# A two-layer decoder trunk on one core: the second layer's input projections by seven products of half-size blocks

## The chip, the cores and the metric

The kernel runs on one core of one Trainium2 chip. A core has five engines with queues of their own: TensorE (PE, matmuls), VectorE (DVE), ScalarE (ACT), GpSimd (POOL) and SyncE (SP, which issues the DMAs here). They wait for each other by semaphores. The metric is the device time of one execution in microseconds, smaller is better. A "product" below is one matmul instruction that streams 512 columns.

## The reference, cut to what matters

One sequence of 1024 tokens, width 1024, float32. Layer 0 is a gated delta rule branch with short convolutions; the change does not touch its arithmetic. Layer 1 is:

```python
def stick_breaking_branch(h, w_in, w_out):           # layer 1; D_MODEL = 1024, 8 heads of 128
    proj = h @ w_in                                  # w_in: 1024 x 4096
    q, k, v, gate = jnp.split(proj, 4, axis=-1)
    ...
    def block(args):                                 # one block of 128 queries, all keys
        mask = key_pos[None, :] < qpos[:, None]
        z = jnp.einsum('bhqd,bhsd->bhqs', q_blk, k).astype(jnp.float32) * scale
        log_1m = jnp.where(mask, jax.nn.log_sigmoid(-z), 0.0)
        tail = lax.cumsum(log_1m, axis=3, reverse=True) - log_1m
        A = jnp.where(mask, jnp.exp(jax.nn.log_sigmoid(z) + tail), 0.0)
        return jnp.einsum('bhqs,bhsd->bhqd', A.astype(v.dtype), v)
    ...
    return (o * jax.nn.silu(gate)) @ w_out

def reference(...):
    u = rmsnorm(h, norm_w[0]); h = h + gated_deltanet_branch(u, ...)
    u = rmsnorm(h, norm_w[1]); h = h + stick_breaking_branch(u, b_w_in[0], b_w_out[0])
    return rmsnorm(h, final_norm_w)
```

## The kernel before, in words

Activations are kept with channels on the 128 partitions and tokens along the free axis: `xT(cb)` is channel block cb (8 of them, 128x1024). Blocks 0 to 4 stay in `home`; 5 to 7 are in `late` and go through DRAM (`resid`) while other data has the memory.

To reach float32 accuracy every projection is made of three products of parts: a factor is split into an upper part (`w_hi`, `u_hi`, a copy of type fp32r) and a rest (`w_lo`, `u_lo`, the difference), and hi*hi + lo*hi + hi*lo are summed in PSUM (`products`). The uppers of weights are copied by ACT (`split_hi`), the rests subtracted by POOL (`split_lo`); weights have two buffers. So one 128x1024 output takes 2 halves x 8 channel blocks x 3 = 48 products, and the four outputs of a head (query, key, gate, value) 192.

At the end of layer 0, `last_group(i)` adds the last two heads' share of the output, 16 groups of 6 products; DVE adds each to xT (`add_output`), ACT makes the upper part of the next layer's input and its squares, DVE the rest (`u_lower_half`), POOL sums the squares (`add_squares`), and PE sums them over the partitions (`block_sum`), from which ACT makes the inverse norm `rsb`. The products of head 0 run meanwhile; the norm is applied behind them (`scale_qk`, `scale_gate`, `scale_v`).

`attend(h)` works on head h in eight steps s, the longest query block (8 blocks of keys) first. On PE a step is: scores of the block two steps ahead, transposes of the weights, their product with the values (`weigh`), and between them products of the next head's projections, in numbers that the table STEP_FILL gives (4 places a step, 192 in all). On DVE a step is: softplus sum, causal mask, a running sum (`scan`), copies of the transposed weights (`copy_aT`), `exponent`; on ACT three functions for softplus, one exponential. Each engine does its instructions in the order in which the code gives them. `take_b` (ACT) brings a finished half of an output from PSUM to `b_raw`, after 24 products each; there are two PSUM banks for projections, 0 and 1. In step 5 DVE scales queries and keys of the next head (`scale_qk`), which PE needs for its scores in step 6. The last head has no next one: PE does the first output block's products in it. After it come the output projection (`products(("out", cb))`, 8 blocks of 48), the final norm, and the store.

## Time and profile before

| | us |
|---|---|
| median of 3 runs | 1469.81 (1467.81 to 1470.13) |
| profiled execution, its own time | 1469.78 |
| its span, first to last instruction | 1468.1 |
| PE busy | 1386.8 (94%) |
| DVE busy | 903.0 (62%) |
| ACT busy | 640.1 (44%) |
| POOL busy | 435.1 (30%) |

The page gives each engine's busy time and the chain of work that ended last, followed back from the end. Layer 0 fills the span to about 776 us (the first `last_group`), the heads of layer 1 run from there to about 1366 us, the output projection to 1449 us. PE's matmuls overlap in the records; the pitch of a row of them says how long one takes.

### The profile page before, as it was taken

What the parts mean: (1) busy time and instruction counts of PE and PEld (TensorE: products, weight loads), DVE (VectorE), ACT (ScalarE), POOL (GpSimd) and SP (SyncE); (2) the same over time, 40 slices, a digit from 0 to 9 for tenths busy, and PEclk for the clock granted to TensorE, in tenths of its full rate; (3) what the DMA queues carried; (4) which work ended last, traced back from release to release, by engine and by line L of the source; (5) the groups of instructions that cost most, each with busy time, mean ns of one, the idle gap of its engine ahead of it and who ended that gap; (6) DMA issues with size and microseconds to landing.
All of it is one profiled execution on the core that took longest, in us unless ns stands there. A gap on an engine that the chain in (4) does not pass through costs nothing.

```text
span 1468.1 us, 18492 instructions
## 1 busy us (share of the span) xinstructions
PE 1386.8 (94%) x7351; PEld 1135.2 (77%) x7351; DVE 903.0 (62%) x1540; ACT 640.1 (44%) x887; POOL 435.1 (30%) x230
## 2 busy tenths in 40 slices
PE   6898999999999999996998999999999999997896
PEld 4687788888888888885886787878787877875785
DVE  7387787869787878777338255454545555557313
ACT  6153435253535353443235354545454454546113
POOL 6542333323333343335124422111212122111120
PEclk9999999999999999997999999999999999999999
DMA  7211110101111101130111201111111111000302
GB/s 188 58 29 29 29 37 22 50 24 37 30 36 37 36 22 37 33 110 27 65 42 57 72 29 44 29 30 29 29 43 29 30 29 40 27 21 0 115 29 114
DMA packets 97190, 65.20 MB, mean 44 GB/s; under 512 B 2401, under 2 KB 91602, under 8 KB 97106
## 3 DMA queue, kind: packets, MB, share of 16 engines
q1 hardware_dynamic: 97106, 64.04, 14.7%
q8 instruction: 58, 0.95, 0.3%
q14 instruction: 26, 0.21, 0.0%
HBM read 53.54 MB, written 10.49 MB: 44 GB/s over the span
## 4 chain that ended last, share of the span: by engine, by line
PE 80%; DVE 12%; POOL 3%; ACT 2%; issue 2%; DMA 0%; POOLq 0%; SPq 0%; DVEq 0%; PEldq 0%; ACTq 0%
PE psum L408 51%; PE psum L1761 4%; PE psum L1787 4%; DVE terms L1316 3%; POOL acc L637 2%; PE psum L1774 2%; PE psum L1704 2%; PE psum L1649 2%; PE psum L1719 2%; PE psum L1674 2%; PE psum L1695 2%; PE psum L1658 1%; DVE small_L L1301 1%; DVE stick L1444 1%; PE psum L1600 1%
## 5 line engine op out<-in xcount | busy, mean ns | idle before, releaser
L408 PE MATMUL psum<-u_hi,w_hi 128*128 128x512 f32 x1264 | 523.9, 414 | 26.0 <-DVE u_lo L1089 7.2
L408 PE MATMUL psum<-u_lo,w_hi 128*128 128x512 f32 x1264 | 517.2, 409 | 0.0
L408 PE MATMUL psum<-u_hi,w_lo 128*128 128x512 f32 x1264 | 506.6, 401 | 0.0
L381 POOL TENSOR_TENSOR w_lo<-w_raw,w_hi 128x1024 fp32r<-128x1024 f32 (+1 forms) x83 | 213.2, 2568 | 702.8 <-ACT w_hi L376 702.8
L408 PEld LDWEIGHTS psum<-u_hi,w_hi 128*128 128x128 f32 x1264 | 240.5, 190 | 81.9 <-issue 19.7
L408 PEld LDWEIGHTS psum<-u_lo,w_hi 128*128 128x128 f32 x1264 | 240.4, 190 | 51.1 <-issue 7.5
L408 PEld LDWEIGHTS psum<-u_hi,w_lo 128*128 128x128 f32 x1264 | 240.2, 190 | 49.8 <-issue 3.8
L376 ACT ACTIVATE w_hi<-w_raw 128x1024 fp32r<-128x1024 f32 (+1 forms) x83 | 85.8, 1034 | 158.7 <-PE psum L408 103.8
L708 POOL TENSOR_TENSOR Lb<-dec,level 128x512 f32<-128x512 f32 (+1 forms) x64 | 89.0, 1406 | 126.5 <-PE psum L1704 69.2
L1185 DVE SCALAR_TENSOR_TENSOR late<-raw,cols,late 128x1024 f32<-128x1024 f32 x72 | 120.1, 1668 | 1.9
L1028 ACT ACTIVATE soft<-psum 128x1024 f32<-128x1024 f32 (+3 forms) x64 | 41.7, 652 | 154.1 <-DVE psum L1432 153.4
L1432 DVE TENSOR_TENSOR psum<-psum,causal 128x128 f32<-128x128 f32 x64 | 19.1, 298 | 132.8 <-PE psum L1761 132.8
L921 ACT ACTIVATE v_new<-psum 128x128 f32<-128x128 f32 x64 | 17.7, 277 | 188.5 <-PE psum L1620 188.5
L1444 DVE TENSOR_TENSOR_SCAN stick<-soft 128x1024 f32<-128x1024 f32 (+3 forms) x64 | 98.3, 1536 | 0.0
L1459 DVE COPY aT<-psum 128x512 f32<-128x512 f32 (+1 forms) x96 | 52.4, 546 | 69.0 <-PE psum L1774 69.0
L1761 PE MATMUL psum<-b_k,b_q 128*128 128x512 f32 (+1 forms) x192 | 74.2, 495 | 8.3 <-DVE stick L1451 7.9
L1787 PEld LDWEIGHTS psum<-aT,b_v 128*128 128x128 f32 x576 | 75.2, 195 | 4.5
L1206 DVE TENSOR_TENSOR raw<-psum,rsb 128x512 f32<-128x512 f32 x64 | 43.8, 687 | 56.6 <-PE psum L408 56.6
L812 ACT ACTIVATE b_raw<-psum 128x512 f32<-128x512 f32 x64 | 38.0, 594 | 91.0 <-PE psum L408 90.9
L1316 DVE TENSOR_TENSOR terms<-Xs,small_T 128x16 f32<-128x16 f32 (+14 forms) x120 | 71.5, 596 | 9.7 <-DVE small_T L1321 0.5
L1787 PE MATMUL psum<-aT,b_v 128*128 128x128 f32 x576 | 76.0, 278 | 0.0
L1761 PEld LDWEIGHTS psum<-b_k,b_q 128*128 128x128 f32 x192 | 34.7, 188 | 32.6 <-issue 15.3
(212 smaller groups left out, 2032.5 us busy)
## 6 DMA issues: line engine op xcount, KB each, us to landing
w_raw<-in_a_w_in SPq DMA_DIRECT2D x33, 512.0 KB, 4.1
w_raw<-in_b_w_in SPq DMA_DIRECT2D x32, 512.0 KB, 4.0
x_stage<-in_x SPq DMA_DIRECT2D x8, 512.0 KB, 7.3
w_raw<-in_b_w_out SPq DMA_DIRECT2D x8, 512.0 KB, 3.6
out<-fin_o SPq DMA_DIRECT2D x8, 512.0 KB, 2.6
resid<-late SPq DMA_DIRECT2D x6, 512.0 KB, 3.4
o_rows<-o_nrm SPq DMA_DIRECT2D x12, 256.0 KB, 2.0
w_raw<-in_a_w_out SPq DMA_DIRECT2D x8, 384.0 KB, 3.2
```

The lines of the kernel that those rows point to most:

```text
L376: A.activation(tiles(w_hi, key), tiles(w_raw, key), ACT.Copy).then_inc(hi_done, 1)
L381: G.tensor_tensor(tiles(w_lo, key), tiles(w_raw, key), tiles(w_hi, key).bitcast(F32), ALU.subtract).then_inc(lo_done, 1)
L408: mm = PE.matmul(psum[:, half], (w_hi, w_hi, w_lo)[part][:, n % 2, k], (u_hi, u_lo, u_hi)[part][:, k, half * HALF:(half + 1) * HALF], star ...
L708: G.tensor_tensor(Lb[:, g, :, used], half_of(dec, g)[:, :, used], level[:, l:l + 1, used].broadcast_to((P, 4, used.stop)), ALU.mult).then_ ...
L1028: A.activation(soft[:, slot, 0:w], banks(bk)[:, 0:w], ACT.Abs).then_inc(soft_a.handle, 1)
L1185: V.scalar_tensor_tensor(out=conv[:, s], in0=tap, scalar=by, in1=conv[:, s], op0=ALU.mult, op1=ALU.add).then_inc(convs.handle, 1)
L1206: V.tensor_tensor(raw[:, slot, 3 + half * HALF:3 + (half + 1) * HALF], psum[:, half], rsb[:, half_range(half)], ALU.mult).then_inc(proj_ta ...
L1316: V.tensor_tensor(terms[:, :, 0:r + 1], row_L[:, r % 2, :, 0:r + 1], small_T[:, :, 0:r + 1], ALU.mult).then_inc(terms_done.handle, 1)
L1444: V.tensor_tensor_scan(stick[:, slot, 0:w][:, ::-1], soft[:, slot, 0:w][:, ::-1], soft[:, slot, 0:w][:, ::-1], 0.0, ALU.add, ALU.bypass).t ...
L1459: V.tensor_copy(aT[:, s % 2, 4 * g:4 * g + n], bank(6, n)).then_inc(at_done.handle, 1)
L1761: mm = PE.matmul(psum[:, bk + c // HALF, 0:n], b_q[:, qb * P:(qb + 1) * P], b_k[:, c:c + n], start=True, stop=True)
L1787: mm = PE.matmul(psum[:, 7, t], b_v[:, blk, :], aT[:, s % 2, blk], start=blk == 0, stop=blk == qb)
```

## The change: what it does

The four projections of a head are taken as two pairs (query and key; gate and value). A pair's output (2 blocks of 128 columns by 2 halves of 512 tokens) is a 2x2 product of blocks over 2 halves of the 1024 channels, and is computed by Strassen's scheme in Winograd's form: seven block products p1 to p7 instead of eight. A block product is 12 matmul products (4 channel blocks x 3 parts), so a pair takes 84 in place of 96. The first pair of all (head 0, query and key) stays plain.

- **Weights.** The left factors of p5, p6, p7 and p3 are sums and differences of weight blocks, made on POOL (`factor_sums`, three 128x512 instructions a pair, and one behind p2's rest). Each of the 14 factors of a head is split at 128x512: `factor_hi` on ACT, `factor_lo` on POOL, in a ring of four.
- **Inputs.** The right factors of p5, p6, p7 and p4 are sums of quarters of the scaled input: made once, on DVE (`difference_t1`, `sums_t`), and split by ACT, DVE and POOL into `t_hi` and `t_lo`, at the start of layer 1. The squares are now taken and added in halves.
- **Results.** The seven products use two PSUM banks and accumulate on each other; ACT takes two results of a pair, DVE five, each with an add (`take_pair`, 128x512).
- **Keys.** The scaled keys of heads 1 to 7 are made on POOL (`scale_k`) in place of DVE.
- **Order in a head.** STEP_FILL has two places a step, 168 in all; in step 7 DVE copies the transposed weights ahead of the scan; in step 0 it scales the values ahead of the copy; ACT's last exponential of a head stands inside the next head's first softplus.
- **Memory.** `o_raw` lies where the input parts are, so outputs of heads 0 to 6 go to DRAM (`b_rows`) and come back in the last head; all eight residual blocks (before: three) are stored and loaded again ahead of the output projection. A barrier at the start of layer 1 is gone.

```diff
-STEP_FILL = ((4, 8, 6, 23), (4, 8, 5, 11), (4, 6, 4, 10), (4, 5, 3, 9), (4, 5, 0, 8), (4, 4, 0, 6),
-             (2, 1, 0, 0), (4, 4, 14, 22))
+STEP_FILL = ((12, 23), (10, 15), (9, 13), (8, 11), (0, 15), (0, 12), (0, 2), (15, 23))
+FIRST_FILL = 6
...
+ORDER = ("p1", "p6", "p2", "p7", "p5", "p4", "p3")
+SECOND_BANK = ("p6", "p7", "p4")
+STARTS = ("p1", "p6", "p5")
+BY_ACT, BY_DVE = ("p1", "p2"), ("p6", "p7", "p5", "p4", "p3")
+PAIRS = 2 * H
+RING = 4
...
+        def pair_bank(p, name):
+            return psum[:, (p - 1 + (name in SECOND_BANK)) % 2]
...
+        def left(f):
...
+            raw = raw_of(p)
+            return {"p1": raw[:, 0, low], "p2": raw[:, 0, high], "p3": raw[:, 0, high], "p4": raw[:, 1, high],
+                    "p5": w_sum[:, 0], "p6": w_sum[:, 1], "p7": raw[:, 1, low]}[name]
...
+        def factor_hi(f):
...
+            else:
+                p, name = (f - 4) // 7 + 1, ORDER[(f - 4) % 7]
+                if name in ("p5", "p6", "p7", "p3"):
+                    A.wait_ge(s_made, 4 * p - 3 + ("p5", "p6", "p7", "p3").index(name))
+                A.wait_ge(pair_in[p % 2], 32 * (p // 2 + 1))
+                A.wait_ge(pair_ready, 3 if f < 6 else 4 if f < 8 else f - RING + 1)
...
+        def factor_sums(p):
...
+            G.wait_ge(pair_in[p % 2], 32 * (p // 2 + 1))
...
+            G.tensor_tensor(w_sum[:, 0], raw[:, 1, low], raw[:, 1, high], ALU.add).then_inc(s_made, 1)
...
+            G.tensor_tensor(w_sum[:, 1], w_sum[:, 0], raw[:, 0, low], ALU.subtract).then_inc(s_made, 1)
+            G.tensor_tensor(raw[:, 1, low], raw[:, 0, low], raw[:, 1, low], ALU.subtract).then_inc(s_made, 1)
+        def factor_lo(f):
+            G.wait_ge(s_hi, f + 1)
+            G.tensor_tensor(ring(w_lo, f), left(f), ring(w_hi, f).bitcast(F32), ALU.subtract).then_inc(s_lo, 1)
+            if f >= 4 and ORDER[(f - 4) % 7] == "p2":
+                G.wait_ge(s_lo, f + 1)
+                G.tensor_tensor(left(f), left(f), w_sum[:, 1], ALU.subtract).then_inc(s_made, 1)
...
+        def pair_products(p, first, last):
...
+                if j == 0 and part == 0:
+                    PE.wait_ge(s_lo, f + 1)
+                    if name in ("p2", "p5"):
+                        PE.wait_ge(pair_act, 2 * p + (3 if name == "p2" else 4))
+                    elif name in ("p7", "p4", "p3"):
+                        PE.wait_ge(pair_dve, 5 * p - 5 + {"p7": 1, "p4": 2, "p3": 3}[name])
+                    elif p > 1:
+                        PE.wait_ge(pair_dve, 5 * p - 5 - (1 if name == "p1" else 0))
+                    else:
...
+                        PE.wait_ge(ub_lo_pool, LO_POOL.index((name, j)) + 1)
+                mm = PE.matmul(pair_bank(p, name), ring((w_hi, w_hi, w_lo)[part], f)[:, j],
...
+            def load_pair(p):
+                if p == 0:
+                    sp.wait_ge(lo_done, NUMBER["last", 1] + 1)
+                elif p == 1:
+                    sp.wait_ge(ub_lo_dve, 1)
+                else:
+                    sp.wait_ge(s_lo, first_of(p - 1))
...
+            sp.wait_ge(pair_ready, FACTORS)
+            for k in range(H - 1):
+                sp.wait_ge(o_out[k % 2], 16 * EARLY + 32 * (k // 2 + 1))
+                sp.dma_start(o_raw[:, k, :], b_rows[k]).then_inc(o_back[k], 16)
...
+            sc_ready.wait(sp, H - 1, NC)
+            for k in (0, 1):
+                sp.dma_start(xT(k), resid[1, k]).then_inc(x_in[k], 16)
+            all_arrived(sp, 2)
+            for k in range(2, KB):
+                sp.dma_start(xT(k), resid[1, k]).then_inc(x_in[k], 16)
...
+            pool.wait_ge(ub_lo_dve, 1)
+            factor_sums(1)
+            add_b_squares(0, 1, KB)
+            factor_lo(0)
+            factor_lo(1)
+            factor_lo(2)
+            factor_lo(3)
+            input_lo("p5")
+            add_b_squares(1, 1, 3)
+            input_lo("p7")
+            for f in range(4, 8):
+                factor_lo(f)
+            input_lo("p4")
+            for n in range(4):
+                add_b_squares(1, n + 3, n + 4)
+                if n < 3:
+                    factor_lo(8 + n)
+            add_b_squares(1, KB - 1, KB)
...
+            def scale_k(h):
...
+                sc_ready.wait(pool, h - 1, NC)
+                G.tensor_tensor(b_k[:, :], b_raw[:, 1], rsb[:, :], ALU.mult).then_inc(bqk_done.handle, 1)
+            factor_sums(2)
+            for f in range(first_of(2), FACTORS):
+                p, g = (f - 4) // 7 + 1, (f - 4) % 7
+                factor_lo(f)
+                if g == 5 and p % 2 == 1:
+                    scale_k(p // 2)
+                if g == 3 and p % 2 == 0:
+                    scale_gate(p // 2 - 1)
+                if g == 4 and p + 1 < PAIRS:
+                    factor_sums(p + 1)
...
+                if half == 0:
+                    input_hi("p1" if cb < HALF_KB else "p2", cb % HALF_KB)
+                    b_square(cb, 0)
+                elif cb < HALF_KB:
+                    scaled_b12(cb)
+                    input_hi("b12", cb)
+                    if cb > 0:
+                        input_hi("p5", cb - 1)
...
+            def b_square(cb, half):
+                r = half_range(half)
+                if cb >= 3:
+                    act.wait_ge(b_acc, half * (KB - 1) + cb - 2)
...
+            def ended_pair(f):
+                p, name = (f - 4) // 7 + 1, ORDER[(f - 4) % 7]
+                if name in BY_ACT:
+                    take_pair(p, name)
+                if f + RING < FACTORS:
+                    factor_hi(f + RING)
...
+            for j in range(HALF_KB):
+                for name in ("p6", "p7"):
+                    input_hi(name, j)
+                if j % 2 == 1:
+                    take_plain(j // 2)
+            for cb in range(3):
+                b_square(cb, 1)
+            take_plain(2)
+            factor_hi(4)
+            factor_hi(5)
+            b_square(3, 1)
+            take_plain(3)
+            factor_hi(6)
+            factor_hi(7)
+            for j in range(HALF_KB):
+                input_hi("p4", j)
+            b_square(4, 1)
+            for f in range(4, 7):
+                ended_pair(f)
+                b_square(f + 1, 1)
             inverse_rms(1)
-            arrive(act)
-            all_arrived(act, 2)
-            def take_b(nh, e):
...
+                V.tensor_tensor(dst, so_far, pair_bank(p, name), ALU.add).then_inc(pair_dve, 1)
...
+                    input_lo("b12", i - KB - 1)
+                    difference_t1(i - KB - 1)
+                if i > KB + HALF_KB:
+                    input_lo("p3", i - KB - HALF_KB - 1)
+            input_lo("p3", HALF_KB - 1)
+            for j in range(HALF_KB):
+                sums_t(j)
+                if j > 0:
+                    input_lo("p6", j - 1)
...
+            ended_pair(5)
+            ended_pair(7)
+            dve.wait_ge(res_out, 16 * (KB - HOME + KB))
+            dve.wait_ge(nrs_done, 2)
+            scale_qk(0)
+            rms_by_tokens(1)
+            ended_pair(8)
             dve.wait_ge(rst_done, 2)
             dve.wait_ge(consts, CONSTS_A + 2)
-            scale_qk(0)
             mask(0, 0)
+            ended_pair(9)
+            mask(0, 1)
             softplus_sum(0, 0)
...
+                ended_pair(14 * h + 10)
                 for s in range(NC):
                     ahead = (h, s + 1) if s + 1 < NC else (h + 1, 0)
                     there = follow or s + 1 < NC
+                    fill.to(STEP_AT[2 * s])
                     if there:
                         softplus_sum(*ahead)
                     if s + 2 < NC:
                         mask(h, s + 2)
                     elif follow:
                         mask(h + 1, s + 2 - NC)
+                    if s == NC - 1:
+                        fill.to(STEP_AT[2 * s + 1] - GROUP)
+                        copy_aT(h, s, 0)
                     if there:
                         scan(*ahead)
-                    copy_aT(h, s, 0)
                     if s == 0:
                         scale_v(h, 0)
+                    if s < NC - 1:
+                        copy_aT(h, s, 0)
                     if there:
                         exponent(*ahead)
+                    fill.to(STEP_AT[2 * s + 1])
                     copy_aT(h, s, 1)
                     if s == 0:
                         scale_v(h, 1)
...
+            plain_products(0, 4 * MMS)
+            pair_products(1, 0, 3 * GROUP)
             block_sum(1)
-            arrive(pe)
-            products(("b", 0, 0), 36, 2 * MMS)
-            products(("b", 0, 1), 0, 2 * MMS)
+            pair_products(1, 3 * GROUP, 4 * GROUP)
             rms_to_tokens(1)
-            products(("b", 0, 2), 0, MMS)
+            pair_products(1, 4 * GROUP, 5 * GROUP)
```

What POOL does at the start of layer 1, before (squares, with the weights of the first head's first outputs between them):

```order
L637 TENSOR_TENSOR acc<-acc,sq 128x1024 [waits sq_done]
L637 TENSOR_TENSOR acc<-acc,sq 128x1024 [waits acc_done,sq_done] x2
L381 TENSOR_TENSOR w_lo<-w_raw,w_hi 128x1024 [waits hi_done]
L637 TENSOR_TENSOR acc<-acc,sq 128x1024 [waits acc_done,sq_done] x4
L381 TENSOR_TENSOR w_lo<-w_raw,w_hi 128x1024 [waits hi_done]
L754 MEMSET causal 128x128 [waits phase]
L626 AFFINE_SELECT causal<-causal 128x128 [waits consts]
```

and after behind the second pair's three weight sums (`w_raw_b` is its buffer, `t_raw` and `o_row` hold input sums):

```order
L945 TENSOR_TENSOR acc<-acc,sq 128x512 [waits b_sq]
L945 TENSOR_TENSOR acc<-acc,sq 128x512 [waits b_acc,b_sq] x6
L538 TENSOR_TENSOR w_lo<-w_raw,w_hi 128x512 [waits s_hi] x4
L952 TENSOR_TENSOR u_lo<-o_raw,u_hi 128x512 [waits ub_hi] x4
L945 TENSOR_TENSOR acc<-acc,sq 128x512 [waits b_acc,b_sq] x2
L952 TENSOR_TENSOR t_lo<-t_raw,t_hi 128x512 [waits ub_hi] x4
L538 TENSOR_TENSOR w_lo<-w_raw_b,w_hi 128x512 [waits s_hi]
L538 TENSOR_TENSOR w_lo<-w_sum,w_hi 128x512 [waits s_hi]
L538 TENSOR_TENSOR w_lo<-w_raw_b,w_hi 128x512 [waits s_hi]
L542 TENSOR_TENSOR w_raw_b<-w_raw_b,w_sum 128x512 [waits s_lo]
L538 TENSOR_TENSOR w_lo<-w_raw_b,w_hi 128x512 [waits s_hi]
L952 TENSOR_TENSOR t_lo<-o_row,t_hi 128x512 [waits ub_hi] x4
```

The squares are in 14 halves, the last of them behind three sums, eleven weight rests and twelve input rests.

What POOL does around the scaled keys of a head, after (before, those four places hold two instructions `w_lo<-w_raw,w_hi 128x1024`):

```order
L538 TENSOR_TENSOR w_lo<-w_sum,w_hi 128x512 [waits s_hi]
L530 TENSOR_TENSOR w_sum<-w_raw 128x512 [waits s_lo,pair_in0]
L532 TENSOR_TENSOR w_sum<-w_sum,w_raw 128x512 [waits s_made]
L533 TENSOR_TENSOR w_raw<-w_raw 128x512
L538 TENSOR_TENSOR w_lo<-w_raw_b,w_hi 128x512 [waits s_hi]
L990 TENSOR_TENSOR b_k<-b_raw,rsb 128x1024 [waits sc_ready,pair_dve,pair_act]
L538 TENSOR_TENSOR w_lo<-w_raw_b,w_hi 128x512 [waits s_hi]
L538 TENSOR_TENSOR w_lo<-w_raw,w_hi 128x512 [waits s_hi]
```

The sums and `b_k` are new here; `b_k` waits for the last scores of the head before.

DVE from step 6 to the end of a head, before (the scaled queries and keys, `b_q` and `b_k`, stand a little ahead of it):

```order
L1444 SCALAR_TENSOR_TENSOR stick<-soft 128x128 [waits sp_done]
L1459 COPY aT<-psum 128x256 [waits at_ready]
L1451 TENSOR_TENSOR stick<-psum,stick 128x128 [waits scan_done]
L1437 SCALAR_TENSOR_TENSOR soft<-psum,soft 128x1024 [waits soft_c]
L1432 TENSOR_TENSOR psum<-psum,causal 128x128 [waits sc_ready]
L1444 SCALAR_TENSOR_TENSOR stick<-soft 128x1024 [waits sp_done]
L1459 COPY aT<-psum 128x128 [waits at_ready]
L1451 TENSOR_TENSOR stick<-psum,stick 128x1024 [waits scan_done]
L1468 TENSOR_TENSOR o_all<-psum,b_g 128x512 [waits bg_done,av_ready]
L1437 SCALAR_TENSOR_TENSOR soft<-psum,soft 128x896 [waits soft_c]
```

and after (`b_raw<-b_raw,psum` takes a block product):

```order
L1816 SCALAR_TENSOR_TENSOR stick<-soft 128x128 [waits sp_done]
L1831 COPY aT<-psum 128x256 [waits at_ready]
L1823 TENSOR_TENSOR stick<-psum,stick 128x128 [waits scan_done]
L1809 SCALAR_TENSOR_TENSOR soft<-psum,soft 128x1024 [waits soft_c]
L1804 TENSOR_TENSOR psum<-psum,causal 128x128 [waits sc_ready]
L1458 TENSOR_TENSOR b_raw<-b_raw,psum 128x512 [waits pair_ready,pair_dve]
L1831 COPY aT<-psum 128x128 [waits at_ready]
L1816 SCALAR_TENSOR_TENSOR stick<-soft 128x1024 [waits sp_done]
L1823 TENSOR_TENSOR stick<-psum,stick 128x1024 [waits scan_done]
L1458 TENSOR_TENSOR b_raw<-b_raw,psum 128x512 [waits pair_ready,pair_dve]
L1841 TENSOR_TENSOR o_row<-psum,b_g 128x512 [waits bg_done,av_ready]
L1458 TENSOR_TENSOR b_raw<-b_raw,psum 128x512 [waits pair_ready,pair_dve] x2
```

Four takes have come in, one ahead of the long scan and three behind it, ahead of the next head's second softplus sum; ahead of this piece `b_q` stands alone.

## Rows read from the trace of the kernel before

**Rows 1.** The page: busy time by engine; the chain that ended last, by engine.

```profile
PE 1386.8 (94%) x7351; PEld 1135.2 (77%) x7351; DVE 903.0 (62%) x1540; ACT 640.1 (44%) x887; POOL 435.1 (30%) x230
...
PE 80%; DVE 12%; POOL 3%; ACT 2%; issue 2%; DMA 0%; POOLq 0%; SPq 0%; DVEq 0%; PEldq 0%; ACTq 0%
```

**Rows 2.** The chain in order of time: start us, us, what.

```profile
933.38 5.25 PE psum L408 x23
...
975.40 2.00 PE psum L1761 x4
...
1307.63 2.00 PE psum L1761 x4
```

**Rows 3.** GpSimd: line L708: duration ns min/median/max; then first start.

```profile
L708 POOL TENSOR_TENSOR Lb<-dec,level x64: 725/1296/2292, 98.9 to 705.7; 128x512 f32<-128x512 f32 x48, 128x256 f32<-128x256 f32 x16
```

**Rows 4.** Timeline of VectorE: start us, us, engine line op out<-in, [idle before].

```profile
849.04 4.46 DVE L1444 TENSOR_TENSOR_SCAN stick<-soft 128x1024 f32<-128x1024 f32 x1
...
970.94 0.30 DVE L1432 TENSOR_TENSOR psum<-psum,causal 128x128 f32<-128x128 f32 x1 [1.05 <-PE psum L1761]
...
973.00 1.22 DVE L1418 SCALAR_TENSOR_TENSOR b_q<-b_raw,rsb 128x1024 f32<-128x1024 f32 x1
...
977.63 1.82 DVE L1444 TENSOR_TENSOR_SCAN stick<-soft 128x128 f32<-128x128 f32 x1
...
982.33 2.28 DVE L1444 TENSOR_TENSOR_SCAN stick<-soft 128x1024 f32<-128x1024 f32 x1
```

**Rows 5.** Timeline of GpSimd, head 0 to head 2, same columns.

```profile
848.95 2.41 POOL L381 TENSOR_TENSOR w_lo<-w_raw,w_hi 128x1024 fp32r<-128x1024 f32 x1 [12.05 <-ACT w_hi L376]
851.32 4.40 POOL L766 TENSOR_TENSOR b_raw<-b_raw,rsb 128x1024 f32<-128x1024 f32 x1
...
976.79 2.38 POOL L381 TENSOR_TENSOR w_lo<-w_raw,w_hi 128x1024 fp32r<-128x1024 f32 x1 [12.89 <-ACT w_hi L376]
```

**Rows 6.** Timeline of VectorE at the start of the second layer.

```profile
782.73 0.74 DVE L1096 SCALAR_TENSOR_TENSOR u_lo<-home,cols,u_hi 128x512 fp32r<-128x512 f32 x1
...
797.54 0.68 DVE L1214 TENSOR_TENSOR home<-psum,home 128x512 f32<-128x512 f32 x1
798.14 2.27 DVE L1096 SCALAR_TENSOR_TENSOR u_lo<-home,cols,u_hi 128x512 fp32r<-128x512 f32 x1
```

**Rows 7.** Timeline of GpSimd at the start of the second layer.

```profile
794.66 7.99 POOL L637 TENSOR_TENSOR acc<-acc,sq 128x1024 f32<-128x1024 f32 x3 [15.88 <-ACT sq L783]
...
805.38 10.97 POOL L637 TENSOR_TENSOR acc<-acc,sq 128x1024 f32<-128x1024 f32 x4
```

**Rows 8.** Timeline of PE (matmuls), start of the second layer and head 1.

```profile
805.47 0.50 PE L408 MATMUL psum<-u_hi,w_hi 128*128 128x512 f32 x1 [2.75 <-POOL w_lo L381]
...
816.41 1.98 PE L1540 MATMUL psum<-acc,ones 128*128 128x512 f32 x4 [0.42 <-POOL acc L637]
...
859.57 1.45 PE L1761 MATMUL psum<-b_k,b_q 128*128 128x512 f32 x4
...
980.02 1.77 PE L1761 MATMUL psum<-b_k,b_q 128*128 128x512 f32 x4 [1.05 <-DVE stick L1451]
```

**Rows 9.** Busy time in one stretch; granted clock is third from the end.

```profile
806.00:811.00 5.00, 4.81 (x14) 3.52 (x13) 3.81 (x3) 1.67 (x2) 4.86 (x2) 0.66 0.29 113
```

**Rows 10.** SyncE: the issue of a weight load, and the time to landing.

```profile
778.81 0.37 SPq L368 DMA_DIRECT2D w_raw<-in_b_w_in  x1
...
w_raw<-in_b_w_in SPq DMA_DIRECT2D x1, 512.0 KB, 4.1
```

**Rows 11.** ScalarE: the norm, and the third output block's weights.

```profile
818.43 1.12 ACT L800 ACTIVATE rsb<-psum,eps_d 128x1024 f32<-128x1024 f32 x1 [5.39 <-PE psum L1540]
...
1378.11 1.06 ACT L376 ACTIVATE w_hi<-w_raw 128x1024 fp32r<-128x1024 f32 x1 [9.99 <-DMA w_raw<-in_b_w_out]
```

**Rows 12.** Window 1340:1468: what the DMA moved in 40 slices of 3.2 us.

```profile
GB/s 0 5 0 0 0 0 0 0 68 325 338 253 4 163 1 164 0 0 74 95 0 0 164 0 0 0 0 0 5 0 0 0 0 0 0 40 348 338 337 248
```

**Rows 13.** VectorE adds the second half of output block 1.

```profile
1383.67 0.69 DVE L1517 TENSOR_TENSOR home<-psum,home 128x512 f32<-128x512 f32 x1 [4.75 <-PE psum L408]
```

471 lines of the change are left out of this document (324 added, 147 removed).

## The prediction, made before the changed kernel ran

> **What bounds the kernel now.** I read the page first. PE is busy 94% of the span and has 80% of the chain that ended last; DVE is at 62%, ACT at 44%, POOL at 30% [rows 1]. Then the chain in order of time over layer 1. It repeats: the scores of the next head's first block start at 975.40 and, five heads later, at 1307.63: five periods of 66.45 us [rows 2]. In it a run of 23 products takes 5.25, so 0.228 us each; 192 of them are 43.8 of the 66.45. Once a head PE waits, 1.05 us, for DVE [rows 8]. So a head is bound by PE.
>
> The start of layer 1 is not. Between the end of layer 0's last groups and head 0's third scores (859.57) PE waits 2.75 us for a weight rest from POOL, and the sum of squares starts (816.41) when POOL has added the last one [rows 8]. After the first of these waits the granted clock is 0.66 over five microseconds [rows 9]: the lower of TensorE's levels for most of it.
>
> Last I looked at POOL and DVE side by side, since the change gives POOL most. A running sum over 128 columns takes 1.82 at 977.63, while POOL's instruction of 976.79 runs to 979.17; one over 1024 takes 4.46 at 849.04 and 2.28 at 982.33 [rows 4, 5]. The POOL instruction behind the one of 848.95, started at 851.32, takes 4.40 instead of 2.4 [rows 5]: each waited for the other's instruction to end, and they took turns. The same for `u_lo`, 0.74 alone and 2.27 beside POOL's adds; but an add that reads PSUM keeps its 0.68 beside them [rows 6, 7]. So DVE instructions with both inputs in SBUF and POOL's share one resource, and each waits at most for the instruction under way.
>
> The Trainium skill ("SBUF — State Buffer", section "SBUF: two separate sides") calls it an exclusive lock on the port pair, held for a whole instruction. If it were a split of bandwidth instead, the turns counted below would cost less and the square sum would come some 4 us sooner. By that rule, the trace agrees: it is taking turns.
>
> **The heads: what goes.** A head has 168 products for 192: 24 x 0.228 = 5.5 us. The wait of 1.05 [rows 8] came from the running sum of 1.82 that met POOL's weight rest [rows 4, 5]; in the new order POOL has nothing under way there, because that factor's copy is made only after ACT has taken p2, and its rest is over before the mask. So 1.05 goes too. An unhindered period is 66.45 - 5.5 - 1.05 = 59.9 us.
>
> **The heads: what comes.** POOL's 128x512 instruction is not in layer 1's rows; half of a 1024 is 1.2 and line L708, the same kind at 512, has a median of 1.30 [rows 3, 5]: I take 1.25. A head gives POOL 14 rests and 8 sums (27.5 us) and two 1024 scalings (4.8): 32 of 60 us, before its turns with DVE. It is no bound as a whole, but where it stands matters.
> - Step 5. The mask behind the last scores is at 970.94, `b_q` at 973.00 (1.22) [rows 4], then `b_k`, and PE's next scores at 975.40 [rows 2]. Before `b_k` POOL now has a rest, three sums and another rest (5 x 1.25 = 6.3, plus turns with two running sums and `b_q`, about 3). Step 4 is 15 products and some 2 us of scores and values, 5.5 in all. Laid from its start, `b_k` ends 6.4 us after step 5 begins; PE, with 12 products in step 5, wants it at 4.4. That is 2.0 us of waiting a head. If all turns fell well it would be 0; with one more long turn, 4.
> - Step 7. DVE's take of p5 stands behind the running sum (2.28) and the exponent (1.2); PE needs it at the start of p3, 12 products after p5. From the mask of the next head, the take ends at 10.0, PE is there at 9.2: 0.9 us. With one POOL turn in the running sum 2.1.
> - Step 0. PE has 12 products ahead of the second transposes of values, where it had 18: 1.4 us less cover for DVE's first scaling of them, and DVE comes 0.6 later (a take of 0.68 with an add, [rows 6]). I take 0.6, from 0 to 1.8.
> - The other takes are half as far apart as before (12 products, 2.7 us, per bank), but DVE is in time for each when I lay its queue beside PE's; two wait at a step's start without holding PE. ACT's 14 copies of 512 for 4 of 1024, less four takes, are 1 to 2 us in an engine at 44%: nothing, as long as the ring of four is ahead.
>
> So a period is 59.9 + 2.0 + 0.9 + 0.6 = 63.4, a gain of 3.0, and 21.4 us in seven heads. Bounds: with no new wait 59.9 (a gain of 46 in seven heads), with each at its upper end (4, 2.1, 1.8) 67.8, a loss of 9. I take values near the middle, since POOL is under way in half of a head and a turn is met by chance.
>
> **The start of layer 1.** I laid the four queues out from 775, in turns where both DVE and POOL read SBUF.
> 1. The second pair's weights are issued when the first `u_lo` of the layer is done, 782.73 + 0.74 = 783.5 [rows 6]. A load lands 4.1 after its issue (778.81 was the one of before) [rows 10]; two, behind the first pair's, I put at 5.5. POOL makes the three sums first: 789.0 + 3.7 = 792.7, and its first add of squares ends at 794.0.
> 2. ACT's squares have two buffers. It now squares from group 3 on in step with the upper parts, so at the fourth square it stands until 794.0. Its next upper parts, DVE's rests and adds behind them, and PE's groups 9 to 16 stand with it, about 8 us. Then each of six more adds alternates with one DVE rest, 1.9 a pair: the seventh ends at 804.8. In before nothing of this held PE, the squares came behind (POOL's first add is at 794.66 [rows 7]).
> 3. In the second half of the groups ACT has three instructions a group for two, DVE three; the first weights' copies come behind the 12th. PE's first product of the layer: 813.8, where it was 805.47 [rows 8].
> 4. From there POOL has 29 instructions to the last add: 36 us, 4 for turns with `sums_t`, and 8 idle at 828 to 836, since the second half's squares stand behind ACT's last upper part of p6, which waits for 13 DVE instructions in turns. The square sum starts at 864, 48 us later than before (816.41). PE has done 132 products by then (30 us) and stands about 11.
> 5. Behind it less is left. The sum itself (1.98 at full clock [rows 8]) I charge at the lower clock, 3.7, since PE has stood; the norm 2.2 (two of 1.12 [rows 11]), `b_q` and `b_k` 2.4 and a turn of 1.2, the scores, mask and softplus 7, then the second mask, softplus sum, running sum and exponent 6.5. Head 0's third scores start at 886.5 instead of 859.57: 27 us later. The work of head 0 is done then in both kernels.
>
> The least of this: no turns, no idle POOL, the load at once. Then the square sum starts at about 845 and PE is the bound, third scores at 867, 7 us late. The most is 33.
>
> **The end.** In the last head POOL makes the output weights' rests and the gate scaling one behind the other, and DVE's long running sums meet them: 1 us. Behind it, the third output block's weights now stand behind six residual loads where there were three. In before they had landed at 1378.11 [rows 11], their rest is done 1.06 + 2.4 later, 1381.6, and PE starts on them when block 1 ends, 0.7 before the add of 1383.67 [rows 13]. A 512 KB load takes 1.55 us at the 338 GB/s of that stretch [rows 12]; three more are 4.7, of which 1.5 are slack: 3.2, and about 1 for the clock behind it [rows 9]. Together 5, between 1 and 8.
>
> **Sum.** The profiled execution took 1469.78 by its own time (span 1468.1), which is the median shown (1469.81). 1469.8 + 27 - 21.4 + 5 = 1480.4. I forecast 1480.
>
> **Rivals.**
> - The start is covered (faster). If POOL's turns are shorter and its queue has no gap, the square sum comes before PE has done its 132 products, that is before about 848, and PE stays the bound: 7 late instead of 27, 1460. For it: POOL's bare work from 789 is 40 x 1.25 = 50 us, ending at 839. Against it: 32 DVE instructions with two SBUF inputs in the same stretch, 0.66 each. It decides whenever the start loses less than 16 us, since heads and end together bring 16.4.
> - The heads run through (faster or the same): new waits under 1 us a head, 59.9 + 0.8, a gain of 40 in seven. With the start as above 1462. For it: DVE has idle time in each step; against it, `b_k` on the engine with the longest queue.
> - Both: 1442.
> - The takes or the ring hold PE (slower yet). If p7's or p5's take or one rest a head comes 2 us late, seven heads lose 14: 1494. For it: takes are due every 2.7 us and stand between DVE's long instructions.
>
> **Chances.** The forecast 0.50 (1473 to 1488), covered start 0.21, heads run through 0.12, both 0.04, held by takes 0.13. Less than 0.2% (2.9 us) either way can't be told from no change: faster, below 1466.9, gets the covered start, both, and half of the third, 0.31; the same 0.11, from the rest of the third and the forecast's lower edge; slower 0.58. The range 1456 to 1494 leaves out "both", a part of the covered start and half of the last.
>
> **What would show it.** The start: the row of the square sum's matmuls (864), PE's idle time before it (11), the first product of the second layer (814), POOL without gaps but one near 830; ACT idle for 8 us at 786 to 794 on POOL's first add. The heads: a period of 63.4, a PE wait at the scores behind `b_k` of about 2 us, one before p3 for a DVE take, no 1.05 before the second scores. The end: a PE wait of 3 us ahead of output block 2. I am wrong if the third scores of head 0 start before 875 or the period is outside 61 to 65.5.

## The result: 0.3% slower, and the profile after

| | before | after |
|---|---|---|
| median, us | 1469.68 (8 runs, 1467.81 to 1470.13) | 1473.65 (8 runs, 1472.23 to 1474.86) |
| ratio after/before, 95% interval | | 1.0030 [1.0019, 1.0041] |
| profiled execution: span, us | 1468.1 | 1471.6 |

The page of the kernel after, busy time by engine and the chain that ended last by engine, answers to [rows 1]:

```profile
PE 1358.8 (92%) x7171; PEld 1104.9 (75%) x7171; DVE 972.4 (66%) x1629; ACT 664.2 (45%) x962; POOL 616.1 (42%) x393
...
PE 70%; DVE 16%; issue 4%; ACT 4%; POOL 4%; DMA 1%; POOLq 0%; SPq 0%; DVEq 0%; PEldq 0%; ACTq 0%
```

PE has 28 us less work, and its share of the chain fell from 80% to 70%: the saved time came back as waiting for POOL, ACT and DVE. The chain in order of time (start us, us, what) says where; the first four rows are the start of the second layer, then come two heads and the end:

```profile
789.74 7.48 issue
...
864.17 3.55 PE psum L1933 x4
...
867.71 2.80 PE psum L596 x12
...
887.18 2.33 PE psum L2153 x4
...
995.26 2.53 DVE b_q L1789
997.84 2.00 PE psum L2153 x4
...
1057.19 2.52 DVE b_q L1789
1059.76 2.00 PE psum L2153 x4
...
1307.36 2.00 PE psum L2153 x4
...
1370.22 11.43 DMA w_raw<-in_b_w_out
```

Head 0's third scores start at 887.18, 27.6 us behind the 859.57 of [rows 8]. The first scores of a head come every 61.9 us (997.84, 1059.76) for 66.45 [rows 2], and at head 7 the kernel has caught up: 1307.36 beside 1307.63 [rows 2], 27.9 gained on the way. Behind that 3.8 are lost again. 27.6 - 27.9 + 3.8 = 3.5 us, the difference of the spans. The periods from head 1 on are 61.94 us in the mean for the first five and 61.77 for the last.

What PE waited for, in total us, times, longest; first the start (770 to 935), then six heads (936 to 1307):

```profile
PE psum L462 <- issue: 11.7, 6, 7.5
PE psum L1933 <- POOL acc L945: 8.6, 1, 8.6
PE psum L596 <- POOL w_lo L538: 4.2, 1, 4.2
...
PE psum L2153 <- DVE b_q L1789: 7.5, 6, 1.3
PE psum L596 <- DVE b_raw L1458: 1.6, 6, 0.3
```

In the start four rows tell the story (POOL, ACT, POOL, POOL; timelines as in [rows 5]):

```profile
789.42 1.26 POOL L530 TENSOR_TENSOR w_sum<-w_raw_b 128x512 f32<-128x512 f32 x1 [10.96 <-DMA w_raw_b<-in_b_w_in]
...
794.49 0.63 ACT L1047 ACTIVATE sq<-home 128x512 f32<-128x512 f32 x1 [9.32 <-POOL acc L945]
...
793.20 10.98 POOL L945 TENSOR_TENSOR acc<-acc,sq 128x512 f32<-128x512 f32 x7
...
835.18 2.74 POOL L945 TENSOR_TENSOR acc<-acc,sq 128x512 f32<-128x512 f32 x2 [8.23 <-ACT sq L1047]
```

POOL stood for the second pair's weights; ACT's squares stood for POOL's adds, and PE's last groups with them; later POOL stood 8.23 us for the second half's squares and had all the rest of its queue still ahead of it. Between 840 and 880 PE is busy for 11.40 and 15.83 of each 20 us. The granted clock is third from the end of these two rows, 0.83 in both:

```profile
840.00:860.00 20.00, 11.40 (x36) 8.74 (x36) 0.69 (x1) 8.12 (x15) 19.92 (x17) 0.83 0.00 1
860.00:880.00 20.00, 15.83 (x62) 11.16 (x63) 5.43 (x7) 6.75 (x8) 11.70 (x11) 0.83 0.20 52
```

And the place in a head where PE waits, DVE and POOL side by side:

```profile
992.59 0.30 DVE L1804 TENSOR_TENSOR psum<-psum,causal 128x128 f32<-128x128 f32 x1 [0.95 <-PE psum L2153]
992.80 1.69 DVE L1816 TENSOR_TENSOR_SCAN stick<-soft 128x256 f32<-128x256 f32 x1
...
995.19 2.60 DVE L1789 SCALAR_TENSOR_TENSOR b_q<-b_raw,rsb 128x1024 f32<-128x1024 f32 x1
```

```profile
988.33 1.76 POOL L530 TENSOR_TENSOR w_sum<-w_raw 128x512 f32<-128x512 f32 x1
...
992.66 1.27 POOL L538 TENSOR_TENSOR w_lo<-w_raw_b,w_hi 128x512 fp32r<-128x512 f32 x1
993.89 2.81 POOL L990 TENSOR_TENSOR b_k<-b_raw,rsb 128x1024 f32<-128x1024 f32 x1
```

DVE meets POOL twice between the mask and the scaled queries: the running sum stands until POOL's rest ends at 993.93, the queries (1.22 alone, [rows 4]) until the keys end at 996.70. The queries, not the keys, are last, and PE goes on 0.05 after them. From the start of the mask to their end DVE needs 5.20 us, and PE waits 1.26.

### The profile page after: what moved, and what is told of

It reads as the page before. It is cut to its first block, busy times and chain, and to the rows that moved or that the text cites. A ratio compares the mean times of both kernels' runs of the same rounds, so it can differ in the third digit from the quotient of the medians.

```text
span 1471.6 us, 18785 instructions
## 1 busy us (share of the span) xinstructions
PE 1358.8 (92%) x7171; PEld 1104.9 (75%) x7171; DVE 972.4 (66%) x1629; ACT 664.2 (45%) x962; POOL 616.1 (42%) x393
## 4 chain that ended last, share of the span: by engine, by line
PE 70%; DVE 16%; issue 4%; ACT 4%; POOL 4%; DMA 1%; POOLq 0%; SPq 0%; DVEq 0%; PEldq 0%; ACTq 0%
PE psum L445 27%; PE psum L596 15%; PE psum L2153 3%; PE psum L2179 3%; DVE terms L1681 3%; DVE stick L1816 2%; PE psum L2097 2%; PE psum L2042 2%; PE psum L2166 2%; PE psum L2112 2%; PE psum L462 2%; PE psum L2067 2%; PE psum L2088 2%; POOL acc L829 1%; DVE b_q L1789 1%
## 5 line engine op out<-in xcount | busy, mean ns | idle before, releaser
L445 PE MATMUL psum<-u_hi,w_hi 128*128 128x512 f32 x752 | 309.4, 411 | 24.6 <-DVE u_lo L1397 6.6
L445 PE MATMUL psum<-u_lo,w_hi 128*128 128x512 f32 x752 | 307.2, 408 | 0.0
L445 PE MATMUL psum<-u_hi,w_lo 128*128 128x512 f32 x752 | 302.1, 402 | 0.0
L416 POOL TENSOR_TENSOR w_lo<-w_raw,w_hi 128x1024 fp32r<-128x1024 f32 (+1 forms) x51 | 122.6, 2405 | 321.4 <-ACT w_hi L411 321.4
L445 PEld LDWEIGHTS psum<-u_hi,w_hi 128*128 128x128 f32 x752 | 143.7, 191 | 58.4 <-issue 15.7
L445 PEld LDWEIGHTS psum<-u_lo,w_hi 128*128 128x128 f32 x752 | 143.8, 191 | 29.9 <-issue 3.8
L445 PEld LDWEIGHTS psum<-u_hi,w_lo 128*128 128x128 f32 x752 | 143.6, 191 | 29.2 <-issue 2.1
L596 PE MATMUL psum<-u_hi,w_hi 128*128 128x512 f32 x240 | 99.4, 414 | 6.1 <-POOL w_lo L538 4.2
L1458 DVE TENSOR_TENSOR b_raw<-b_raw,psum 128x512 f32<-128x512 f32 x75 | 51.2, 683 | 81.0 <-PE psum L596 81.0
L596 PE MATMUL psum<-u_hi,w_lo 128*128 128x512 f32 x240 | 96.4, 402 | 0.0
L596 PE MATMUL psum<-u_lo,w_hi 128*128 128x512 f32 x240 | 96.3, 401 | 0.0
L538 POOL TENSOR_TENSOR w_lo<-w_raw,w_hi 128x512 fp32r<-128x512 f32 x39 | 52.1, 1338 | 102.4 <-ACT w_hi L522 101.7
L538 POOL TENSOR_TENSOR w_lo<-w_raw_b,w_hi 128x512 fp32r<-128x512 f32 x40 | 56.3, 1406 | 78.5 <-ACT w_hi L522 77.8
```

What stands on the lines that cost most here:

```text
L416: G.tensor_tensor(tiles(w_lo, key), tiles(w_raw, key), tiles(w_hi, key).bitcast(F32), ALU.subtract).then_inc(lo_done, 1)
L445: mm = PE.matmul(psum[:, half], (w_hi, w_hi, w_lo)[part][:, n % 2, k], (u_hi, u_lo, u_hi)[part][:, k, half * HALF:(half + 1) * HALF], star ...
L538: G.tensor_tensor(ring(w_lo, f), left(f), ring(w_hi, f).bitcast(F32), ALU.subtract).then_inc(s_lo, 1)
L596: mm = PE.matmul(pair_bank(p, name), ring((w_hi, w_hi, w_lo)[part], f)[:, j], right(*((u_hi, t_hi), (u_lo, t_lo), (u_hi, t_hi))[part], nam ...
L1458: V.tensor_tensor(dst, so_far, pair_bank(p, name), ALU.add).then_inc(pair_dve, 1)
```

## The experiments

Each kernel ran beside the kernel before on the same chip. Ratios are to before; what an edit is worth is read against the changed kernel's 1473.65, which was measured in an earlier group of runs; the median of the kernel before lay between 1469.46 and 1469.68 in all groups.

### 1. Squares before sums

```diff
-            factor_sums(1)
             add_b_squares(0, 1, KB)
+            factor_sums(1)
```

> POOL adds the first half's squares before it makes the second pair's three sums, as in the kernel before; nothing else of the changed kernel is touched. Theory (the wait for the second pair's weights blocks the squares, and by the two square buffers the last groups): ACT's idle of 9.3 us at 785 and PE's idle of 7.5 us at 790 go, PE keeps its clock there, and the layer's first product starts about 8 us sooner (806 for 814.6). The square sum then comes 6 to 8 us sooner, since POOL's queue behind it is the same but for the turns: 1466 to 1468 us in all. Rival (POOL's queue from there on sets the square sum, and its gap before 835 only grows): the first product comes sooner, the square sum within 2 us of 864, and the time stays at 1472 to 1474.

1467.97 us, ratio 0.9984 [0.9976, 0.9993]: 5.7 less, by this one exchange. The 9.3 of ACT and the 7.5 of PE are gone, and the layer's first product starts at 809.51 for 814.62. The chain of this kernel:

```profile
859.10 3.78 PE psum L1933 x4
862.88 3.84 PE psum L596 x12
```

The square sum is 5.1 sooner (859.10 for 864.17), not 6 to 8; the three sums now meet DVE's instructions (1.72, 1.61, 1.72 for 1.26 each), which is part of it. In this execution the 12 products behind it took 3.84 for 2.80 (above, 867.71), with a granted clock of 0.72 from 862.9 to 866.7, which gave 1 us back. This execution is the slowest of twelve, at 1470.80; the fastest took 1465.27. So the wait was real, and the median lies at the upper edge of the 1466 to 1468 expected.

### 2. Output weights ahead of the residual

```diff
+            for n in (2, 3):
+                load_w(sp, ("out", n), wbo_v[:, :, n * P:(n + 1) * P])
             for k in range(2, KB):
                 sp.dma_start(xT(k), resid[1, k]).then_inc(x_in[k], 16)
...
-            for n in range(2, KB):
+            for n in range(4, KB):
```

> SP issues the loads of the output projection's weight blocks 2 and 3 ahead of the residual loads 2 to 7, everything else is as in the changed kernel. Theory (block 2's weights stand behind six residual loads, 11.4 us of ACT's wait at 1370, and PE waits for their rest): the rest of block 2 is done before PE ends block 1, PE's idle before 1385 goes, 3 to 4 us less: 1469.5 to 1471. Rival (the residual adds, which then come two loads later, hold the PSUM banks and so PE): the time stays within 1 us of 1473.6, and DVE waits for the residual at the end instead.

1470.32 us, ratio 1.0005 [0.9996, 1.0013]: 3.3 less, inside the 3 to 4 expected. ACT's copy of block 2, and PE's run in the chain:

```profile
1374.11 1.06 ACT L411 ACTIVATE w_hi<-w_raw 128x1024 fp32r<-128x1024 f32 x1 [4.41 <-DVE home L1909]
```

```profile
1371.08 29.11 PE psum L445 x120
```

The weights are no longer what ACT waits for (the chain above had 11.43 us of DMA there), PE runs through blocks 1 and 2, and no residual add is late.

### 3. Keys on DVE in every head

```diff
-                if g == 5 and p % 2 == 1:
-                    scale_k(p // 2)
...
-                if h == 0:
+                if True:
                     V.tensor_tensor(b_k[:, :], b_raw[:, 1], rsb[:, :], ALU.mult)
```

> DVE scales the keys in every head, behind the queries, as it does in the first head and in the kernel before; POOL scales none. Theory (the scaled keys are not late on POOL, it is the queries' turn behind them that PE waits for): queries at 995.2 take 1.2 alone, the keys on DVE 1.2 to 2.4 behind them, so PE starts the scores at 997.7 to 998.8 where it now starts at 997.84: period 62.0 to 63.0, time 1473.5 to 1480. Rival (POOL's load is what costs, the keys on it most): the period falls to 60.9 or less and the time to 1467 or less.

1471.17 us, ratio 1.0009 [1.0000, 1.0017]: 2.5 less, where I expected 0 to 6 more; the rival's 1467 wasn't reached either. DVE in the same place:

```profile
992.37 1.69 DVE L1814 TENSOR_TENSOR_SCAN stick<-soft 128x256 f32<-128x256 f32 x1
...
994.76 1.21 DVE L1787 SCALAR_TENSOR_TENSOR b_q<-b_raw,rsb 128x1024 f32<-128x1024 f32 x1
995.89 1.21 DVE L1790 TENSOR_TENSOR b_k<-b_raw,rsb 128x1024 f32<-128x1024 f32 x1
```

The two together take 2.34 with no turn, and are done 0.25 sooner after the mask than the queries alone that stood for POOL's keys. The next head's scores start at 997.16 and the one's after at 1058.89, a period of 61.7, 0.2 less. Moving the keys to POOL bought nothing: POOL takes 2.39 for what DVE does in 1.21, and DVE waits for it anyway.

Nearly half of the 2.5 comes from one place that the expectation did not single out. Ahead of head 7 no further pair has sums, so POOL's rest of p4 is over before the mask, and with the keys on DVE nothing of POOL is under way there:

```profile
1301.01 0.68 DVE L1814 TENSOR_TENSOR_SCAN stick<-soft 128x256 f32<-128x256 f32 x1
```

The running sum takes 0.68, PE doesn't wait at the scores, and this period is 60.7 (1244.08 to 1304.79) for 61.8 in the changed kernel.

### 4. Keys before the weight rest

```diff
+                if g == 5 and p % 2 == 1:
+                    scale_k(p // 2)
                 factor_lo(f)
-                if g == 5 and p % 2 == 1:
-                    scale_k(p // 2)
```

> POOL scales the keys one instruction earlier, before the weight rest of p4 and not behind it. Theory (the queries, last of the two, wait for the keys' end on POOL and for nothing else): keys end 1.2 us sooner, at 995.5, the queries need one short turn at most, and PE's wait of 1.26 a head at the scores goes: period 60.8, 7 to 8 us less in seven heads, 1466 us. Rival (the keys then meet DVE's running sum of 256, which comes later by as much, or p4's products wait for their rest): period 61.7 to 62.3 and a time within 2 us of 1473.6.

1474.25 us, ratio 1.0029 [1.0019, 1.0039]: no gain, the theory failed and its rival held, with a period of 62.0. DVE:

```profile
991.84 2.86 DVE L1816 TENSOR_TENSOR_SCAN stick<-soft 128x256 f32<-128x256 f32 x1
...
995.40 1.46 DVE L1789 SCALAR_TENSOR_TENSOR b_q<-b_raw,rsb 128x1024 f32<-128x1024 f32 x1
```

The queries have almost no turn (1.46 for 2.60), but the running sum stands through the whole 2.39 us of the keys, 2.86 for 1.69, and the queries end as late after the mask (5.23 for 5.20). Exchanging the two instructions of POOL moved DVE's loss from the queries to the running sum and did not make it smaller.

### 5. Another order for the start

```diff
+            add_b_squares(0, 1, KB)
             factor_sums(1)
-            add_b_squares(0, 1, KB)
-            factor_lo(0)
-            factor_lo(1)
-            factor_lo(2)
-            factor_lo(3)
-            input_lo("p5")
-            add_b_squares(1, 1, 3)
-            input_lo("p7")
-            for f in range(4, 8):
-                factor_lo(f)
-            input_lo("p4")
-            for n in range(4):
-                add_b_squares(1, n + 3, n + 4)
-                if n < 3:
-                    factor_lo(8 + n)
-            add_b_squares(1, KB - 1, KB)
+            for f in range(4):
+                factor_lo(f)
+            add_b_squares(1, 1, 3)
+            input_lo("p5", 0, 4)
+            add_b_squares(1, 3, 6)
+            input_lo("p7", 0, 2)
+            add_b_squares(1, 6, 7)
+            factor_lo(4)
+            factor_lo(5)
+            add_b_squares(1, 7, KB)
...
```

Behind these come, in POOL's queue, the rests of the weights 6 to 10 with the inputs of p7 and p4 between them. ACT makes three squares of the second half (`b_square(cb, 1)`) ahead of its waits for DVE's t inputs, and one behind each of them, where all stood behind the last of them or later.

> The second layer's start alone is put in another order: POOL adds the first half's squares before the sums, and adds each square of the second half as soon as ACT has made it; ACT squares the second half while it waits for DVE's t inputs; the rests follow in the order in which PE takes the products; heads and end are as in the changed kernel. Theory (POOL's and ACT's order, not POOL's load, makes the square sum late, and behind it little hides the chain): the last add ends near 836 and not at 864, PE starts the square sum after its 132 products at about 843, never waits for it, and head 0's third scores start near 865 for 887: 18 us less, 1455 us. Rival (POOL's load from 789 on is what counts: 40 instructions of 1.25 and their turns end at the same time in any order): the wait moves from the square sum to the weight rests of p7 to p4, third scores not before 880, time 1466 to 1470.

1458.16 us, ratio 0.9922 [0.9908, 0.9935]: 15.5 less, of 18 expected, and faster than before the change. Its chain:

```profile
828.18 6.62 issue
...
850.60 1.72 PE psum L1935 x4
...
871.39 0.70 PE psum L2155
```

The same instructions on the same engines, and the square sum starts at 850.60 for 864.17, with no wait for POOL; the third scores at 871.39 for 887.18. In the stretch from 840 to 860 the granted clock, third from the end, is 1.00; it was 0.83 (above):

```profile
840.00:860.00 20.00, 20.00 (x92) 15.65 (x91) 5.27 (x6) 9.28 (x15) 17.60 (x16) 1.00 0.01 3
```

The edit contains run 1's exchange, worth 5.7; the other 9.8 are the second half's squares and the order of the rests, which were not tried apart. The square sum was expected at 843; ahead of it PE has a new wait, 6.6 us at 828, before the fourth plain group.

### 6. Keys on DVE, and POOL's rest behind them

The edit of run 3, and in POOL's loop:

```diff
+                if g == 5 and p % 2 == 1:
+                    bqk_done.wait(pool, p // 2, 2)
```

> DVE scales the keys behind the queries in every head (as in the run with the keys on DVE), and POOL's weight rest of p4 in the same step waits until both are scaled. Theory (DVE's chain from the mask to the scaled keys is what PE waits for, and each POOL instruction that it meets there adds about 1.1 us): the running sum of 256 takes 0.6 for 1.69, the keys end 1.1 sooner, PE's wait of 1.0 goes, period 60.7, and the time is 7 us below the 1471.2 of the keys on DVE alone: 1464. Rival (the rest of p4, now 4 us later, holds its products or the ring behind it): period 61.7 or more and 1470 or more.

1466.13 us, ratio 0.9972 [0.9962, 0.9983]: 5.0 below run 3, 7.5 below the changed kernel. DVE, then PE's waits over six heads:

```profile
992.76 0.68 DVE L1816 TENSOR_TENSOR_SCAN stick<-soft 128x256 f32<-128x256 f32 x1
...
994.13 1.22 DVE L1789 SCALAR_TENSOR_TENSOR b_q<-b_raw,rsb 128x1024 f32<-128x1024 f32 x1
995.26 1.22 DVE L1792 TENSOR_TENSOR b_k<-b_raw,rsb 128x1024 f32<-128x1024 f32 x1
```

```profile
PE psum L596 <- DVE b_raw L1458: 1.1, 6, 0.2
```

With POOL quiet for 4 us the running sum takes 0.68, the wait at the scores is gone, and the period is 60.8 (scores at 996.54 and 1057.33; six periods from 935.79 to 1300.34). The rest, made 4 us later, held nothing. This is the theory's mechanism: 0.97 us a period (61.73 for 60.76), but only in the five periods where run 3 still had the wait, which makes 4.8 and not the 7 expected. It is the only one of the four edits in a head (runs 3, 4, 6, 7) that took POOL out of the stretch in every head.

### 7. No sums

```diff
-            G.tensor_tensor(w_sum[:, 0], raw[:, 1, low], raw[:, 1, high], ALU.add).then_inc(s_made, 1)
+            n = KB // 2 if p == 1 else 1
+            G.tensor_tensor(w_sum[:, 0, 0:n], raw[:, 1, 0:n], raw[:, 1, 4:4 + n], ALU.add).then_inc(s_made, 1)
...
```

> From the third pair on POOL's three sums of weights take 128 columns for 512 each; so most of the sums of the weights is left out, and the output is not the reference's. All else, keys on POOL too, is as in the changed kernel. It takes 2.9 us of POOL's work out of each pair, 5.8 of a head. Theory (not POOL's load but the one instruction that it has under way when DVE scans and scales counts): the keys then start at the last scores, meet the running sum of 256, and the queries end as late: period 61.4 to 62.1, time 1469 to 1474. Rival (the load sets PE's wait): the wait at the scores goes, period 60.7 or less, 1464 or less.

1471.32 us, ratio 1.0013 [1.0004, 1.0022], 2.3 less than the changed kernel, and in the theory's range. Though POOL has some 5 us less to do in each head, the queries are still what PE waits for, 1.1 us a head:

```profile
990.67 2.39 POOL L991 TENSOR_TENSOR b_k<-b_raw,rsb 128x1024 f32<-128x1024 f32 x1 [0.15 <-PE psum L2154]
```

```profile
990.74 2.86 DVE L1817 TENSOR_TENSOR_SCAN stick<-soft 128x256 f32<-128x256 f32 x1
```

Period 61.75 for 61.94: about 1 us in all six, so the rest of the 2.3 lies outside the periods. With the keys on POOL, its load is not the cost: the keys start at the last scores, as in run 4, and meet the running sum. The queries then take 1.21, without a turn, and end 4.99 after the start of the mask. The changed kernel itself shows it once: ahead of head 7 no further pair has sums, and there the running sum takes 2.87, the queries 1.21, and PE waits 1.1. With the keys on DVE it is different: in that same place of run 3, where POOL has no sums to make, its rest of p4 is over at 1300.79, the mask starts at 1300.80, and the wait is gone. That is seen in one head only and was not tried in the others.

### 8. All four edits

Runs 5, 2 and 6 in one kernel.

> The new order of the start, the output weights 2 and 3 ahead of the residual, the keys on DVE and POOL's rest of p4 behind them, all in one. Theory (the parts lie one behind the other on PE's path, so they add up): 18 from the start, 3 from the end, 2.5 and 7 from the heads: about 1443 us. Rival (they share one gain, PE's clock or the same waits, or a new wait comes at the end): above 1450.

1446.03 us, ratio 0.9842 [0.9829, 0.9855]. The parts were worth 15.5, 3.3 and 7.5, in sum 26.3; together 27.6. They add up, as parts do that lie on PE's path at places of their own; the expected 1443 had the start at 18 and the heads at 9.5.

### 9. One step further in the start

ACT takes the plain groups' banks one step sooner, POOL makes the rests of p1 and p6 before its last three adds, and DVE makes the input rests of p4 and of half of p7:

```diff
-            add_b_squares(1, 3, 6)
-            input_lo("p7", 0, 2)
-            add_b_squares(1, 6, 7)
+            add_b_squares(1, 3, 5)
             factor_lo(4)
             factor_lo(5)
-            add_b_squares(1, 7, KB)
+            add_b_squares(1, 5, 7)
+            input_lo("p7", 0, 2)
...
```

> The version with all four edits, and on top: ACT takes the plain groups' banks one t-step sooner (PE stood 2.2 and 5.0 us at 822 and 835 for them), POOL makes the rests of p1 and p6 before it adds the last three squares, and DVE, which stood 12 us at 837, makes the input rests of p4 and half of p7 in place of POOL. Theory (these two waits are all that holds PE from 809 to the square sum, now that POOL has room): the plain groups end at 832 for 843, the square sum starts near 841 for 851.6, 8 to 10 us less: 1437 us. Rival (POOL and DVE share SBUF in turns, so work given from one to the other costs as much, and DVE's t chain, in turns with POOL until 836, sets p6 and the last add): the square sum not before 848, 1443 us or more.

1440.04 us, ratio 0.9816 [0.9794, 0.9837]: 6.0 below run 8 and 29.4 below before, the lowest median here. Its five times are 1438.43, 1439.20, 1440.04, 1444.73 and 1446.35: the upper two are no better than run 8's (1445.72 to 1447.66), and why they differ was not tried. The profiled execution is the one of 1439.20. In its chain:

```profile
823.31 1.71 DVE t_raw L1430
...
842.66 1.70 POOL acc L948
...
844.41 1.98 PE psum L1938 x4
```

The plain groups end at 831.0 (832 expected, 843.4 in run 8), but the square sum is only 7.2 sooner than in run 8 (851.64), not 10: behind the plain groups PE now stands 4.4 us in three waits, 2.5 of them for a weight rest of POOL, and DVE and POOL are both in turns there, 1.7 for 0.75 and 1.25. So the two waits went as the theory said, and the turns that the rival named took part of it back.

## Why the prediction was right and wrong, point by point

- **The start: right.** Third scores of head 0 at 887.18, 27.6 late; the prediction had 886.5 and 27. Its steps hold one by one, as it gave them in brackets: the sums at 789.42 (789.0), the adds' end at 804.2 (804.8), the square sum at 864.17 (864), POOL's idle stretch at 827 to 835 (828 to 836), PE's wait for it 8.6 (11). The difference in the last is a wait of 4.2 for the rest of p1's weights ahead of it, which was not in the list. The turns were counted as exclusive; run 9's rows (1.7 for 0.75) and the agreement of the sum bear that out. The terms behind the square sum add to 23.0, which from 864 gives 887.0 and not the 886.5 written; the measured stretch is 23.0. The first rival (a covered start) fell, but only by the order: in run 5 the same work leaves the third scores 11.8 us late, which is less than the 16 at which that rival decides.
- **The end: right within its range.** 3.8 us for 5, of which the output weights are 3.3 (run 2); expected for them were 4.2 with the clock. PE's wait ahead of output block 2 is 2.0 for the 3 named.
- **The heads, what goes: 0.5 too much.** The period without the two waits is 61.94 - 1.26 - 0.27 = 60.4 for 59.9, and run 6, less its wait of 0.2, has 60.6. So 24 products and the wait of 1.05 gave 6.0 and not 6.55. About 0.3 of it stands in the rows: in unbroken runs the products of the heads start 0.232 us apart in the mean, for 0.230 before, which is 0.3 in 168. Why, and where the rest is, was not tried.
- **The heads, what comes: this is the step that failed, by size.** Predicted were 2.0 + 0.9 + 0.6 = 3.5 us a head; measured 1.26 at the scores, 0.27 at the take of p5 (the second row of six heads' waits), and nothing at the values: 1.5. That is 2.0 a head too much, and with the 0.5 above against it 1.45 is left in the period (61.94 for 63.4), 9 us in the six full periods. Of these 2.4 were lost again in what is left of head 0 behind its third scores, which gained only 0.7 (48.7 for 49.4 us to head 1's first scores) and was put down as a full one. That leaves 6.5 less than forecast in the heads; with 0.6 more at the start and 1.2 less at the end it is the 7 us between the forecast (10.6 more than before) and the spans (3.5 more). The mechanism at step 5 was the one named (a turn with the keys and what stands before them), but I charged 3 us of turns between POOL's rest of p5 and the end of the keys. The rows show 0.5 in the first sum (1.76 for 1.25) and 0.4 in the keys: the other instructions of POOL kept their 1.27 to 1.30, since DVE works from PSUM or waits there. With all five turns charged the keys came out at 11.9 us after step 4 begins; they end 10.0 after it.
- **What bounds the wait was not seen.** I took the keys for the last of the two. Runs 3, 4, 6 and 7 show that it is DVE's own chain, from the start of the mask to the last scaled instruction on DVE. PE's wait follows its length, whichever way it is made long (run 3 with one meeting and the keys' own 1.21, run 7 with one long meeting, run 4 and the changed kernel with two):

  | | chain on DVE, us | PE waits, us |
  |---|---|---|
  | run 4 | 5.23 | 1.3 |
  | changed kernel | 5.20 | 1.26 |
  | run 7 | 4.99 | 1.1 |
  | run 3 | 4.94 | 1.0 |
  | run 6 | 3.93 | 0 |

  The rival that the heads run through (60.7 a period) is what run 6 made.
- The direction held, and the last rival (held by takes) fell: of the ten takes that DVE does for a head's two pairs only one of p5 makes PE wait, 0.3 us.

So the change itself is a gain of 4.5 us a head, paid for by the queue orders that it came with. With its instructions in other places of the queues, the keys back on DVE and six of POOL's input rests on DVE too, it is 1.8% faster than before (interval 1.6 to 2.1%), and not 0.3% slower; run 8, without the input rests, is 1.6% faster (1.4 to 1.7%).

## What to carry to other kernels

Lay queues out beside each other in time, but charge a turn only where the other engine has an instruction of the sharing kind in just that moment; here a turn charged to each came out at 3 us where 0.9 was found. When work moves to a less busy engine that shares a resource with the old one, ask less how loaded it is than what it has under way while the old engine walks the chain that PE waits for, and keep it quiet there. Where a kernel's start loses what its loop gains, look for one early wait in an in-order queue: exchanging two lines (run 1) was worth more than the whole loss.

## What the runs showed of the hardware

- DVE and POOL take turns with operands in SBUF, instruction by instruction: the same running sum of 256 columns took 0.68 with POOL quiet, 1.69 behind the end of a 1.27 instruction and 2.86 behind one of 2.39 (runs 6, 3 and 4). The Trainium skill ("SBUF — State Buffer", section "SBUF: two separate sides") calls it an exclusive lock that the instruction which starts first holds for its whole length. The traces agree, with these sizes.
- POOL's multiplication of 128x1024 took 2.39 (run 7), DVE's 1.21 (run 3), without a turn in both cases.
- An idle spell of PE can cost more behind it, and not always the same. After 8.9 us of idle and the square sum in run 1, the next 12 products took 3.84 us, at a granted clock of 0.72; after 8.6 us in the changed kernel the same 12 took 2.80, at 1.00. Run 1's times spread over 5.5 us, those of runs 2 and 3 over 2.8 and 3.2; that this is the cause was not tried.
